# Feed-forward strips of gate and up as seven block products instead of eight

## The chip, the cores and the metric

The kernel runs on one core of a Trainium2 chip. The metric is the time of one execution on the device, in microseconds (us). TensorE multiplies matrices (PE in the profile, its weight loads PEld), VectorE (DVE) and ScalarE (ACT) work on elements, GpSimd (POOL) does little here, and SyncE (SP) issues the DMAs that bring weights from memory.

## The reference, cut to what matters

Two transformer blocks over 512 tokens of width 1024 in fp32. There are three feed-forwards of hidden width 2816. The first (f = 0) has a causal convolution between its products and is not touched. The second and third (f = 1 and f = 2) are the gated ones of the second block:

```python
def swiglu(h, w_gate, w_up, w_down):
    return (jax.nn.silu(h @ w_gate) * (h @ w_up)) @ w_down
```

Before each stands a norm with a shift and a scale that come from a product of the conditioning vector with `w_mod`, which the kernel calls `mod`.

## The kernel before

Activations lie transposed: features on the 128 partitions, 512 tokens along a row. Each fp32 operand is cut in a high part (fp32r, a copy by ScalarE) and a low part (the rest, a subtraction by VectorE). A product of two operands is three matmuls: high by high, high by low, low by high (`three`). All accumulate in one bank of `ps`.

The work is a fixed list of 'units'. A unit is one strip of weights, 128 output features by all input tiles (8 tiles of 128), times 512 tokens: 8 x 3 = 24 matmuls with 512 columns each into bank u % 2. The 22 hidden tiles of a feed-forward come in three parts of 8, 8 and 6. A part does for each hidden tile t a gate strip and an up strip, then the 8 strips of the down product over the hidden tiles of the part (`FF_PARTS`, stage names `(f, "up", part)` and `(f, "down", part)`).

The loop bodies per hidden tile are:

- SP loads strip u into slot u % 4 of `w_raw` when unit u - 4 is done.
- ScalarE `cut_hi(u + 2)` and `cut_hi(u + 3)` copy strips to `w_hi`; it takes silu of the gate's bank into `t_b`, and later copies `t_b` to `y_hi`.
- VectorE `cut_lo(u + 2)` and `cut_lo(u + 3)` subtract into `w_lo`; it multiplies `t_b` by the up bank and subtracts `y_lo = t_b - y_hi`.
- TensorE runs `unit(u)` and `unit(u + 1)`. It waits for the strip's low part (`lo_cut`) and for its bank having been read (`bank_read`).

In the down stage VectorE adds each strip's bank to `x` (`residual`). In f = 1, part 0, VectorE also sums up the third group of `mod` there (`mod_sum`), and after the norm `mix2`, which follows f = 1, it sums the fourth. For that TensorE turns tiles of `mod_acc` (`mod_turn(3)`, 16 transposes) just behind the totals of that norm, and then runs `keep_busy(6, 0)`, six idle matmuls of 256 columns, until the first normed tile is there.

Each engine works through its own list in order. Nothing but semaphores ties them. The two buffers `w_raw` and `w_lo` of a slot share their memory, so the low part is written over the raw strip.

## Time and profile before

| | |
|---|---|
| time, median of 3 runs | 1790.01 us (1788.58 to 1790.34) |
| time of the profiled execution | 1788.7 us |
| its span, first to last instruction | 1786.8 us |
| granted TensorE clock | 1.000 of full speed |
| PE busy, share of the span | 99% |
| DVE busy | 56% |
| ACT busy | 38% |

The span is what the trace shows between the first and the last instruction of the core, and the time of an execution is 1.9 us more. In the views a group's duration is that of one instruction from its start to its modelled end. Instructions of one engine overlap at their edges, so what one costs in a packed stream is the distance from its start to the next one's start.

### The profile page before, as it was taken

How to read it: one execution, taken by the hardware profiler on the slowest of the kernel's cores; microseconds unless marked ns; L12 is line 12 of the kernel's file. 1: busy time of each engine (PE TensorE's matmuls, PEld its weight loads, DVE VectorE, ACT ScalarE, POOL GpSimd, SP SyncE). 2: the span in 40 equal slices, each digit the busy share in tenths (PEclk: the TensorE clock that was granted, in tenths of full speed). 3: DMA queues.
4: the chain of work that ended last, by engine and by line, in shares of the span. 5: the costliest groups of instructions: out<-in, count | busy, mean ns of one | idle time of the engine just before them, and what ended most of it. 6: DMA issues, size and time to landing. Idle time of an engine off the chain costs nothing. (4 is left out here: it accounts for less than half of the span.)

```text
span 1786.8 us, 20550 instructions
## 1 busy us (share of the span) xinstructions
PE 1775.4 (99%) x8453; PEld 1480.8 (83%) x8453; DVE 992.1 (56%) x1384; ACT 676.4 (38%) x1041; POOL 23.4 (1%) x54
## 2 busy tenths in 40 slices
PE   8999999999999999999999999999999999999999
PEld 8888888887888888888888888888888888888887
DVE  5755553457787766684433333768878633333333
ACT  5544441334323322352222222465666432122222
POOL 0000000000000000000000000001100000000000
PEclk9999999999999999999999999999999999999999
DMA  5323232355586555333233333232221333333333
GB/s 161 112 85 92 83 86 86 102 187 165 191 260 227 193 188 192 94 96 102 86 102 95 95 95 91 74 83 60 55 64 36 95 106 95 96 101 98 94 89 100
DMA packets 326609, 201.64 MB, mean 113 GB/s; under 512 B 7112, under 2 KB 315766, under 8 KB 326518
## 3 DMA queue, kind: packets, MB, share of 16 engines
q1 hardware_dynamic: 326082, 199.52, 37.3%
q8 instruction: 67, 1.10, 0.3%
q0 software_dynamic: 192, 0.52, 0.1%
q10 hardware_dynamic: 244, 0.30, 0.0%
q14 instruction: 24, 0.20, 0.0%
HBM read 196.39 MB, written 2.10 MB: 111 GB/s over the span
## 5 line engine op out<-in xcount | busy, mean ns | idle before, releaser
L1560 PE MATMUL ps<-u_hi,w_hi 128*128 128x512 f32 (+1 forms) x1664 | 647.8, 390 | 4.6 <-DVE u_lo L1119 2.1
L1560 PE MATMUL ps<-u_hi,w_lo 128*128 128x512 f32 (+1 forms) x1656 | 641.3, 387 | 0.0
L1560 PE MATMUL ps<-u_lo,w_hi 128*128 128x512 f32 (+1 forms) x1664 | 637.9, 387 | 0.0
L955 DVE TENSOR_TENSOR w_lo<-w_raw,w_hi 128x1024 fp32r<-128x1024 f32 (+2 forms) x306 | 363.3, 1187 | 244.0 <-ACT w_hi L511 242.6
L511 ACT ACTIVATE w_hi<-w_raw 128x1024 fp32r<-128x1024 f32 (+2 forms) x307 | 314.6, 1025 | 236.3 <-DMA w_raw<-in_w_down 80.0
L1560 PEld LDWEIGHTS ps<-u_hi,w_hi 128*128 128x128 f32 x1664 | 312.5, 188 | 70.2 <-DVE w_lo L955 4.6
L1560 PEld LDWEIGHTS ps<-u_lo,w_hi 128*128 128x128 f32 x1664 | 312.6, 188 | 62.4
L1560 PEld LDWEIGHTS ps<-u_hi,w_lo 128*128 128x128 f32 x1656 | 310.9, 188 | 63.7
L1560 PE MATMUL ps<-y_hi,w_hi 128*128 128x512 f32 (+1 forms) x662 | 257.1, 388 | 0.0
L1560 PE MATMUL ps<-y_hi,w_lo 128*128 128x512 f32 (+1 forms) x662 | 256.4, 387 | 0.0
L1560 PE MATMUL ps<-y_lo,w_hi 128*128 128x512 f32 (+1 forms) x662 | 256.3, 387 | 0.0
L1560 PEld LDWEIGHTS ps<-y_hi,w_lo 128*128 128x128 f32 x662 | 124.3, 188 | 25.4
L1560 PEld LDWEIGHTS ps<-y_lo,w_hi 128*128 128x128 f32 x662 | 124.3, 188 | 25.2
L1560 PEld LDWEIGHTS ps<-y_hi,w_hi 128*128 128x128 f32 x662 | 124.3, 188 | 25.1
L720 ACT ACTIVATE y_hi<-t_b 128x512 fp32r<-128x512 f32 x66 | 41.8, 633 | 239.8 <-DVE t_b L1309 239.8
L1032 DVE SCALAR_TENSOR_TENSOR x<-ps,gains,x 128x512 f32<-128x512 f32 (+1 forms) x59 | 42.5, 723 | 138.1 <-PE ps L1560 138.1
L1309 DVE TENSOR_TENSOR t_b<-t_b,ps 128x512 f32<-128x512 f32 x66 | 45.2, 685 | 111.9 <-PE ps L1560 111.9
L1093 DVE SCALAR_TENSOR_TENSOR mod_acc<-mod_raw,c_act,mod_acc 128x1024 f32<-128x1024 f32 x63 | 80.7, 1281 | 3.4 <-DVE mod_acc L1093 0.5
L717 ACT ACTIVATE t_b<-ps 128x512 f32<-128x512 f32 x44 | 26.4, 599 | 138.5 <-PE ps L1560 138.5
L1311 DVE TENSOR_TENSOR y_lo<-t_b,y_hi 128x512 fp32r<-128x512 f32 x66 | 45.7, 693 | 46.1 <-ACT y_hi L720 46.1
L545 ACT ACTIVATE t_b<-x 128x512 f32<-128x512 f32 x28 | 17.7, 632 | 83.8 <-DVE x L1030 47.2
L1030 DVE TENSOR_TENSOR x<-x,ps 128x512 f32<-128x512 f32 (+1 forms) x34 | 22.1, 654 | 33.2 <-PE ps L1560 32.8
(290 smaller groups left out, 1319.6 us busy)
## 6 DMA issues: line engine op xcount, KB each, us to landing
mod_raw<-in_w_mod SPq DMA_DIRECT2D x72, 512.0 KB, 4.8
w_raw<-in_w_in SPq DMA_DIRECT2D x71, 512.0 KB, 3.9
w_raw<-in_w_ffn_up SPq DMA_DIRECT2D x44, 512.0 KB, 3.9
w_raw<-in_w_gate SPq DMA_DIRECT2D x44, 512.0 KB, 3.8
w_raw<-in_w_up SPq DMA_DIRECT2D x44, 512.0 KB, 3.8
w_raw<-in_w_down SPq DMA_DIRECT2D x32, 512.0 KB, 3.8
w_raw<-in_w_ffn_down SPq DMA_DIRECT2D x16, 512.0 KB, 3.8
w_raw<-in_w_down SPq DMA_DIRECT2D x16, 384.0 KB, 3.4
```

The costliest lines, as they stand in the source:

```text
L511: e.activation(w_hi[u % SLOTS][:, 0:n_k, :], w_raw[u % SLOTS][:, 0:n_k, :], ACT.Copy).then_inc(hi_cut, 1)
L545: e.activation(t_b[c % 2][:, :], x[:, c, :], ACT.Square).then_inc(squared, 1)
L717: e.activation(t_b[j][:, :], ubank(u), ACT.Silu).then_inc(bank_read[u % 2], 1)
L720: e.activation(y_hi[:, t, :], t_b[j][:, :], ACT.Copy).then_inc(y_hi_set, 1)
L955: e.tensor_tensor(w_lo[u % SLOTS][:, 0:n_k, :], w_raw[u % SLOTS][:, 0:n_k, :], f32(w_hi[u % SLOTS][:, 0:n_k, :]), ALU.subtract).then_inc(l ...
L1030: ins = e.tensor_tensor(x[:, c, cols], x[:, c, cols], src[:, cols], ALU.add)
L1032: ins = e.scalar_tensor_tensor(out=x[:, c, cols], in0=src[:, cols], scalar=gain(c), in1=x[:, c, cols], op0=ALU.mult, op1=ALU.add)
L1093: e.scalar_tensor_tensor(out=acc, in0=r, scalar=c_act[:, k:k + 1], in1=acc, op0=ALU.mult, op1=ALU.add).then_inc(mod_taken, 1)
L1309: e.tensor_tensor(t_b[j][:, :], t_b[j][:, :], ubank(u + 1), ALU.mult).then_inc(bank_read[(u + 1) % 2], 1)
L1311: e.tensor_tensor(y_lo[:, t, :], t_b[j][:, :], f32(y_hi[:, t, :]), ALU.subtract).then_inc(y_lo_set, 1)
L1560: return e.matmul(out_, lhsT, rhs, start=start, stop=stop, skip_group_check=skip)
```

## The change

Of the 44 pairs of gate and up strips in f = 1 and f = 2, 29 (`PAIRS`) are computed in another way. The two strips are seen as a 2 x 2 block matrix: gate or up, times upper or lower half of the input features (`KH` = 4 tiles each). The activations are 2 x 2 blocks too: upper or lower half of the features, times first or second half of the tokens (256 columns). The four result blocks then come from seven block products (Winograd's form of Strassen's scheme) in place of eight. Each product is 4 x 3 = 12 matmuls of 256 columns. For it sums of weight blocks (four a pair) and sums of activation blocks (four a feed-forward, `t_raw`) are formed, cut in high and low parts, and results are added after.

The pairs run in five runs, one each in f = 1 parts 1 and 2 and in f = 2 parts 0, 1 and 2, of 7, 5, 5, 7 and 5 pairs. Before each run one regular tile (three in f = 2, part 0) stays (`PLAIN_TILES`). Two sets of pair buffers alternate. Set 1 lies on the memory of the four weight slots, so its first load waits for the last regular unit, and the down strips' first loads wait for the run's last but one pair. The products 4 and 3 of a pair are issued after 1 and 2 of the next one. Those of a run's last pair are issued within its first down unit.

`mod_turn(3)` moves from the norm `mix2` to a place before the last down unit of f = 1, part 0; the sums of `mod`'s fourth group move there too, since the activation sums take the memory of `mod_acc`. `keep_busy` of that norm grows from 6 to 20. The waits on unit counters are rewritten with helpers (`units_before`, `banks_read`, `slot_loads`) that leave the paired units out; this changes no order elsewhere.

The core of the diff:

```diff
+PLAIN_TILES = {1: (8, 1, 1), 2: (3, 1, 1)}
+RUNS = [(f, p) for f in (1, 2) for p in range(3) if PLAIN_TILES[f][p] < FF_PARTS[p]]
+PAIRS = [(f, p, t) for f, p in RUNS for t in range(PLAIN_TILES[f][p], FF_PARTS[p])]
...
         def sync(e):
+            def load_gate(q):
...
+                name, c, _, _ = UNITS[PAIR_UNIT[q]]
+                e.dma_start(entries(st_raw[n], spot(q).w11, 2).rearrange("p (k n) -> p k n", n=P), strip(PAIR_UNIT[q])).then_inc(gate_in[n], 16)
...
+            def load_pairs(run):
...
+                    e.wait_ge(t_set, 4)
+                load_gate(first)
+                load_up_top(first)
+                load_up_bottom(first)
+
+                e.wait_ge(unit_done, units_before(PAIR_UNIT[first]))
+                load_gate(first + 1)
+                load_up_top(first + 1)
+                load_up_bottom(first + 1)
+                load_gate(first + 2)
+                for q in range(first + 2, last + 1):
+                    load_up_top(q)
+                    if q < last:
+                        load_gate(q + 1)
+                    load_up_bottom(q)
...
         def scalar(e):
+            def pairs(f, part):
+                first, last = FIRST_PAIR[f, part], LAST_PAIR[f, part]
+                for q in range(first, last + 1):
+                    if q > first:
+                        part_sums(q)
+                        part_second(q)
+                    e.wait_ge(product_done, nth_product(q, 1))
+                    if q:
+                        e.wait_ge(up_1, q)
+                    e.activation(q1_sb, pair_bank(q, 0), ACT.Copy).then_inc(kept, 1)
+                    part_last(q)
+                    if q < last:
+                        part_gate(q + 1)
+                    e.wait_ge(gates_set, nth_half(q, 0))
+                    e.activation(pair_tile(q)[:, half(0)], pair_tile(q)[:, half(0)], ACT.Silu).then_inc(hidden_act, 1)
+                    if q == last:
+                        cut_hi(U[f, "down", part])
+                    if q > first:
+                        second_silu(q - 1)
+                    e.wait_ge(product_done, nth_product(q, 6))
+                    if q > 1:
+                        e.wait_ge(gates_set, nth_half(q - 2, 1))
+                    e.activation(t_sb(q), pair_bank(q, 0), ACT.Copy).then_inc(kept, 1)
...
+                    if q > first:
+                        finish(q - 1)
+                    e.wait_ge(product_done, nth_product(q, 5))
+                    e.activation(q1_sb, pair_bank(q, 2), ACT.Copy).then_inc(kept, 1)
...
         def vector(e):
+            def pairs(f, part):
+                first, last = FIRST_PAIR[f, part], LAST_PAIR[f, part]
+                for q in range(first, last + 2):
+                    before, ahead = q > first, q <= last
+                    last_sum = f == 2 and part == 0 and q == first
+                    if before:
+                        up_second(q - 1)
+                    if before and ahead:
+                        add_last(q)
+                    if q - 2 >= first:
+                        low_hidden(q - 2)
+                    if before and ahead:
+                        part_second(q)
+                        part_sums(q)
+                    if ahead:
+                        first_gate(q)
+                        part_last(q)
+                    if before:
+                        up_first(q - 1)
+                        second_gate(q - 1)
+                    if q < last:
+                        part_gate(q + 1)
...
+                    if before:
+                        hidden(q - 1)
+                    if q < last:
+                        add_strips(q + 1)
...
         def tensor(e):
+            def product(q, n, dst, left, right, start):
+
+                for k in range(KH):
+                    ins = three(pair_bank(q, dst), (left[0][:, k, :], left[1][:, k, :]), (right[0](k), right[1](k)), start and k == 0, True, skip=True)
+                ins.then_inc(product_done, 1)
...
+                for q in range(first, last + 1):
...
+                    product(q, 1, 0, (hi[:, spot(q).w11, :, :], lo[:, spot(q).low11, :, :]), block_of(0, 0), True)
+                    product(q, 2, 1, (hi[:, spot(q).w12, :, :], lo[:, spot(q).low12, :, :]), block_of(KH, 0), True)
+                    if q > first:
+                        fourth_product(q - 1)
+                        third_product(q - 1)
...
+                    product(q, 6, 0, (hi[:, spot(q).s2, :, :], hi[:, spot(q).s2_raw, :, :]), sum_of(1), False)
...
+                    product(q, 5, 2, (hi[:, spot(q).s1, :, :], lo[:, spot(q).s1, :, :]), sum_of(0), True)
...
+                    product(q, 7, 0, (hi[:, spot(q).s3, :, :], lo[:, spot(q).s3, :, :]), sum_of(2), False)
...
+                        if f == 1 and part == 0 and c == KC - 1:
+                            mod_turn(3)
...
             total("mix2")
-            mod_turn(3)
-            keep_busy(6, 0)
+            keep_busy(20, 0)
```

What VectorE's steps are, with the elements of a row: `add_strips` three sums of 512, `add_last` one of 512, `part_gate`, `part_sums` and `part_last` one subtraction of 1024 each, `part_second` one of 512, `up_second`, `first_gate` and `second_gate` one sum of 256 each, `up_first` and `hidden` one product of 256 each, and `low_hidden` a subtraction of 512. In the regular tile before a run `beside_plain` does `add_strips`, `add_last`, `part_gate`, `part_second` and `part_sums` of the first pair, ahead of that tile's own multiplication. The activation sums (`whole`, `token_sum`, `token_low`: four of each, 1024 elements) stand beside the down units of f = 1, part 0, and around the three regular tiles of f = 2, part 0.

## Rows read from the trace of the kernel before

**Rows 1.** The page: busy time of each engine; granted clock in 40 slices

```profile
PE 1775.4 (99%) x8453; PEld 1480.8 (83%) x8453; DVE 992.1 (56%) x1384; ACT 676.4 (38%) x1041; POOL 23.4 (1%) x54
...
PEclk9999999999999999999999999999999999999999
```

**Rows 2.** TensorE's waits, the longest: us in total, times, longest

```profile
PE ps L1560 <- DVE u_lo L1119: 2.1, 1, 2.1
```

**Rows 3.** Chain that ended last, a piece of f = 2: start us, us, what

```profile
1420.22 334.86 PE ps L1560 x1476
```

**Rows 4.** Timeline, last unit, columns halved: start us, us, engine, instruction

```profile
1778.30 0.28 PE L1560 MATMUL ps<-y_lo,w_hi 128*128 128x256 f32 x1
1778.30 0.19 PEld L1560 LDWEIGHTS ps<-y_hi,w_lo 128*128 128x128 f32 x1
...
1780.20 0.28 PE L1560 MATMUL ps<-y_hi,w_lo 128*128 128x256 f32 x1
```

**Rows 5.** Timeline of TensorE early in the kernel, columns halved

```profile
27.26 0.28 PE L1560 MATMUL ps<-u_lo,w_hi 128*128 128x256 f32 x1
...
29.88 0.28 PE L1560 MATMUL ps<-u_hi,w_lo 128*128 128x256 f32 x1
```

**Rows 6.** VectorE's groups by form: count, busy us, mean ns, idle before

```profile
L955 DVE TENSOR_TENSOR w_lo<-w_raw,w_hi 128x1024 fp32r<-128x1024 f32 x274 | 334.8, 1222 | 211.4 <-ACT w_hi L511 210.4
L1093 DVE SCALAR_TENSOR_TENSOR mod_acc<-mod_raw,c_act,mod_acc 128x1024 f32<-128x1024 f32 x63 | 80.7, 1281 | 3.4 <-DVE mod_acc L1093 0.5
L1311 DVE TENSOR_TENSOR y_lo<-t_b,y_hi 128x512 fp32r<-128x512 f32 x66 | 45.7, 693 | 46.1 <-ACT y_hi L720 46.1
...
L1359 DVE TENSOR_TENSOR v_hi<-ps,v_hi 128x256 fp32r<-128x256 f32 x16 | 6.0, 419 | 1.0 <-ACT v_hi L759 0.8
...
L1032 DVE SCALAR_TENSOR_TENSOR x<-ps,gains,x 128x256 f32<-128x256 f32 x6 | 2.7, 481 | 6.1 <-PE ps L1560 6.1
```

**Rows 7.** Timeline of VectorE: packed pairs of instructions, in two stages

```profile
706.30 1.22 DVE L955 TENSOR_TENSOR w_lo<-w_raw,w_hi 128x1024 fp32r<-128x1024 f32 x1 [1.65 <-ACT w_hi L511]
707.44 0.68 DVE L1309 TENSOR_TENSOR t_b<-t_b,ps 128x512 f32<-128x512 f32 x1
...
1156.26 2.48 DVE L1049 TENSOR_REDUCE mod<-ps 128x4 f32<-128x512 f32 x4
```

**Rows 8.** ScalarE's groups by form

```profile
L511 ACT ACTIVATE w_hi<-w_raw 128x1024 fp32r<-128x1024 f32 x275 | 289.6, 1054 | 231.6 <-DMA w_raw<-in_w_down 78.7 <-DMA w_raw<-in_w_ffn_down 41.8 <-DMA w_raw<-in_w_gate 35.1
...
L759 ACT ACTIVATE v_hi<-ps 128x256 fp32r<-128x256 f32 x16 | 5.3, 382 | 1.0 <-PE ps L1563 0.8
```

**Rows 9.** DMA issues: count, KB each, median us to landing; then slots until 40 us

```profile
w_raw<-in_w_gate SPq DMA_DIRECT2D x44, 512.0 KB, 3.8
...
w_raw<-in_w_attn_out SPq DMA_DIRECT2D x8, 256.0 KB, 2.8
...
DMA to landing us min/median/max: 3.7/6.7/9.8
```

**Rows 10.** Timeline of TensorE in the norm `mix2`

```profile
1144.03 1.91 PE L1563 MATMUL ps<-consts,mod_acc 128*128 128x128 f32 x16
1145.70 0.96 PE L1560 MATMUL ps<-mask_win,ones_r 128*128 128x256 f32 x6
1146.74 0.47 PE L1560 MATMUL ps<-u_hi,w_hi 128*128 128x512 f32 x1
```

**Rows 11.** Timeline of VectorE in the regular tiles of f = 2, part 0

```profile
1429.07 0.75 DVE L989 SCALAR_TENSOR_TENSOR u_lo<-t_a,mod,u_hi 128x512 fp32r<-128x512 f32 x1
1432.79 1.23 DVE L955 TENSOR_TENSOR w_lo<-w_raw,w_hi 128x1024 fp32r<-128x1024 f32 x1 [2.97 <-ACT w_hi L511]
...
1442.31 0.69 DVE L1309 TENSOR_TENSOR t_b<-t_b,ps 128x512 f32<-128x512 f32 x1 [2.63 <-PE ps L1560]
1443.70 0.69 DVE L1311 TENSOR_TENSOR y_lo<-t_b,y_hi 128x512 fp32r<-128x512 f32 x1 [0.70 <-ACT y_hi L720]
...
1453.19 0.69 DVE L1309 TENSOR_TENSOR t_b<-t_b,ps 128x512 f32<-128x512 f32 x1 [2.64 <-PE ps L1560]
```

More of the change, by code:

```diff
@@ L250, in two_blocks @@
             ctx.push(r1.pop_all())
+        pair_tiles(0, 16)
+        with ExitStack() as r2:
+            wholes = {1: [sb(f"u_whole{n}", [P, KH, SEQ], F32, r2) for n in range(2)]}
         with ExitStack() as r2:
@@ L701, in ffn @@
                     y0 = Y_FILL[f, part]
-                    for t in range(tiles):
+                    for t in range(PLAIN_TILES[f][part] if f else tiles):
                         j = t % 2
@@ L1042, in residual @@
                         mod_sum(2, c)
+                    if u0 == U[1, "down", 0]:
+                        if c == KC - 1:
+                            for k in range(MOD_BANKS[3]):
+                                mod_sum(3, k)
+                        beside_down(c)
                 if u0 == U[1, "down", 0]:
                     mod_finish(2)
+                    mod_finish(3)
             def mod_sum(g, k):
@@ new lines, in add_last, with beside_plain @@
+            def add_last(q):
+                n = pair_set(q)
+                e.wait_ge(blocks_summed, 2 * q + 1)
+                if q > 1:
+                    e.wait_ge(product_done, nth_product(q - 2, 3))
+                e.tensor_tensor(entries(st_raw[n], spot(q).s4), entries(st_sum[n], spot(q).s2_raw), entries(st_raw[n], spot(q).w12), ALU.add).then_inc(blocks_summed, 1)
+            def beside_plain(f, part, t):
+                sums = f == 2 and part == 0 and t == 2
+                if sums:
+                    token_sum(f, 2)
+                if (f, part) in RUNS and t == PLAIN_TILES[f][part] - 1:
+                    first = FIRST_PAIR[f, part]
+                    add_strips(first)
+                    add_last(first)
+                    if sums:
+                        token_low(f, 2)
+                    part_gate(first)
+                    part_second(first)
+                    part_sums(first)
@@ new lines, in behind_plain @@
+            def behind_plain(f, part, t):
+                if f == 2 and part == 0 and t == 0:
+                    whole(f, 2)
+                    whole(f, 3)
+                    token_sum(f, 0)
+                    token_sum(f, 1)
+                elif f == 2 and part == 0 and t == 1:
+                    token_sum(f, 3)
+                    token_low(f, 0)
+                    token_low(f, 1)
+            def pairs(f, part):
[20 more added lines that the diff above has]
+                        part_gate(q + 1)
+                    elif q == last:
+                        cut_lo(U[f, "down", part])
+                    if last_sum:
+                        token_low(f, 3)
+                    if before:
+                        hidden(q - 1)
+                    if q < last:
+                        add_strips(q + 1)
+                    elif q == last:
+                        cut_lo(U[f, "down", part] + 1)
+                low_hidden(last)
@@ L1294, in ffn @@
                     y0 = Y_FILL[f, part]
-                    for t in range(tiles):
+                    for t in range(PLAIN_TILES[f][part] if f else tiles):
                         j = t % 2
@@ L1335, in vector @@
             norm("mix2", U["gate_f"])
-            for k in range(MOD_BANKS[3]):
-                mod_sum(3, k)
-            mod_finish(3)
             p0 = U["proj"]
@@ L1802, in ffn @@
                         unit_pair(U[f, "up", 0], u_act, FILL[f"ffn{f}"] * KC)
-                    for t in range(2 if part == 0 else 0, 2 * tiles):
+                    for t in range(2 if part == 0 else 0, 2 * (PLAIN_TILES[f][part] if f else tiles)):
                         unit(U[f, "up", part] + t, u_act)
+                    if (f, part) in RUNS:
+                        pairs(f, part)
                     if f == 2 and part == 2:
```

433 lines of the change are left out of this document (368 added, 65 removed).

## The prediction

> **What bounds the kernel now.** I read the page first, then TensorE's waits, then the chain, then single stretches of the timeline. The page shows TensorE busy for 1775.4 of 1786.8 us, at the full granted clock in every slice [rows 1]; VectorE and ScalarE are busy for about half of the span or less. The reader should see that one engine is the bound. The waits agree: the longest that TensorE ever has is 2.1 us, at the very start [rows 2], and all its waits together are 8.3 us. In the chain the whole of f = 2 up to its last down strips is one piece of TensorE, 334.86 us for 1476 matmuls [rows 3]. So what counts is first how much time TensorE's own stream loses, and then whether any other engine can still follow.
>
> **TensorE's stream, the gain.** A piece of 1476 matmuls with 512 columns in 334.86 us is 0.2269 us for one [rows 3]. A regular pair of strips is 2 x 24 = 48 of them, 10.89 us. The new pair is 7 x 12 = 84 matmuls of 256 columns, each with weights of its own. The kernel has some of just this kind. In its last unit two of them stand 16 places apart, at 1778.30 and 1780.20, so one takes 0.1188 us [rows 4]; early in the kernel two stand 22 apart, at 27.26 and 29.88, 0.1191 us [rows 5]. Half the columns thus cost 0.52 of the time, not 0.50. With 0.119 a new pair takes 10.00 us. The gain is 0.89 us a pair, and 29 x 0.894 = 25.9 us. A count of work alone, an eighth of 10.89, would have given 39.5 us; the third that is missing is what narrow matmuls lose.
>
> The weight load of one of these matmuls is shown 0.19 us long, more than the 0.119 us between matmuls [rows 4], and yet the stream doesn't slow down; loads overlap with the matmuls and with each other. The Trainium skill (TensorE: Matmul & The Clock Gate, Part 3, 'The mechanism') says that a weight load overlaps with running matmuls only where it is for another group of rows, which would speak against the change; the row contradicts it. The same page ('Back-to-back issue gap') gives N / 2.4 + 2.5 ns between matmuls. By it I estimate 48 x 215.8 - 84 x 109.2 ns = 1.19 us a pair and 34 us in all; the rows have 227 and 119 ns, and the sum goes by them.
>
> **What is moved onto the path.** `mod_turn(3)` stood in the norm `mix2`, where TensorE has nothing to do until the first normed tile. Its 16 transposes run from 1144.03 to 1145.70, 1.67 us [rows 10]. Now they stand between two down units of f = 1, in the full stream, and cost that and about 0.1 us for the restart of the matmuls: 1.8 us. In the norm `keep_busy(20)` fills 20 x 0.119 = 2.4 us from 1144.03 and ends at 1146.4; the first real matmul is at 1146.74 [rows 10]. So it costs nothing. VectorE's four reductions that leave that norm, 2.5 us [rows 7], had no one waiting, and I count nothing for them.
>
> **VectorE in a steady pair.** This is the term that can undo the change. VectorE's packed instructions overlap by 0.08 us: one of 1.22 us is followed after 1.14 [rows 7]. From the forms [rows 6] less 0.08, the three subtractions of 1024 cost 3 x 1.14; the three sums of `add_strips` 0.72 (its successor waits for it) + 0.61 + 0.61; `add_last`, `part_second` and `low_hidden` 3 x 0.61; the three small sums 3 x 0.35 and the two small products 2 x 0.40. Together 3.42 + 1.94 + 1.83 + 1.05 + 0.80 = 9.04 us, against TensorE's 10.00. It fits, with 0.96 to spare.
>
> Does the order of its list allow it? Let TensorE start product 1 of pair q at 0, and each product take 1.43. A result can be read 0.33 us after its last slot. Product 7 of pair q - 1 can be read at 0.3. Then `up_second` to `up_first` cost 0.35 + 0.61 + 0.61 + 0.61 + 1.14 + 0.35 + 1.14 + 0.40 = 5.21, until 5.5. `second_gate` has to wait for product 3, readable at 5.7 + 0.3 = 6.0. It and `part_gate`, `hidden` and `add_strips` cost 3.83, until 9.9; the next product 7 can be read at 10.3. Both idle times are short, 0.5 and 0.4 us. TensorE's own needs come later than VectorE's results: product 4 at 2.9 wants `up_second` (0.7), product 6 at 5.7 wants `part_second` (2.6), the next product 1 at 10.0 wants `part_gate` (7.7). The nearest is product 7 at 8.6. It wants ScalarE's copy of product 6's bank, readable at 7.5, copied by 7.9; the copy stands behind `second_silu`, which ends at 6.0 + 0.42 + 0.39 = 6.9. So 0.7 us are left. ScalarE's own sum is about 5.5 us: three copies of 1024 at 0.96, two of 512 at 0.54, five small ones at 0.3 [rows 8]. I take a steady pair at 10.00.
>
> **The edges of the five runs.** Here other engines do show.
>
> - Set 1 lies on the weight slots, so the second pair's gate strip is asked for only when the last regular unit is done. It lands after 3.8 us [rows 9]; ScalarE's `part_gate` makes that 4.9, the silu and the copy of product 6 behind it 5.7. Product 7 of the first pair is due after four products, at 5.7. I take 0.1 us a run, 0.5 in all.
> - f = 1, part 1: VectorE comes late from the down units. Behind the last one it has `residual` 0.67, four reductions 2.5, two `token_low` 2.3 and two `mod_finish` of about 0.5, 6.0 to 6.5 us, and then 5.5 us of preparation before the regular tile's multiplication. ScalarE's copy of product 1 is queued behind that tile's `y_hi`. Product 6 then waits for 0.3 us.
> - f = 2, part 0: four `whole`, four `token_sum` and three `token_low` stand before the run. The first two `whole` fit into 2.97 us of idle time [rows 11]. The next four sums move the second tile's multiplication from 1442.3 to 1443.0, `y_lo` then ends at 1445.0, three more bring VectorE to 1448.5. From there `token_sum` 1.14, `add_strips` 1.94, `add_last` 0.61, `token_low` 1.14 and `part_gate` 1.14 end at 1454.5. Product 1 is due at about 1453.0, just ahead of the third multiplication at 1453.19 [rows 11]. TensorE waits for 1.5 us, and for 0.4 again at product 6: 1.9.
> - Ends of the runs: from product 3 of the last pair 0.33 + 0.42 + 0.39 + 0.48 + 0.63 + 0.69 and five hand-overs of 0.03 make 3.1 us to `y_lo`. In the parts of 6 tiles it is covered by 12 matmuls, 2.7 us: 0.4 us each, twice. In those of 8 tiles 15 matmuls, 3.4 us, cover it.
>
> Sum: 0.5 + 0.3 + 1.9 + 0.8 = 3.5 us. Bounds: nothing, if VectorE is a little quicker everywhere; three times as much, some 10 us, if each edge has one more instruction of 1.2 us in front. The down strips that follow a run are asked for a whole pair ahead, 10 us against 3.8, and cost nothing.
>
> **The number.** 25.9 - 1.8 - 3.5 = 20.6 us less. The profiled execution took 1788.7 us (1786.8 of span and 1.9 around it), the median of the runs 1790.0, 1.3 more. 1788.7 - 20.6 + 1.3 = 1769.4, and I say 1769.5.
>
> **Rivals.**
>
> A. VectorE doesn't overlap here, because nearly each of its instructions waits for another engine's semaphore. Then full durations count: 3 x 1.222 + 6 x 0.693 + 3 x 0.419 + 2 x 0.481 = 10.05, with 14 hand-overs of 0.03 10.5 us [rows 6]. VectorE becomes the bound by 0.5 us a pair, in the pairs of a run behind its second, 19 of them: + 9.5, 1779. For it speaks how little is spare; against it the packed instruction in [rows 7], which also had a semaphore. The Trainium skill (VectorE: DVE Perf Modes, 'Terms') has a flush behind each operation, the next one starting only when the pipe is empty, which would be this case; the 1.14 us after a 1.22 us instruction disagree.
>
> B. The first loads of set 1 pile up. The second pair's gate strip has two halves of the up strip and another gate strip right behind it on the queue. In the pile-up at the start of the kernel a slot took 6.7 us at the median, up to 9.8 [rows 9]. 2.9 us more in each of five runs are + 14.5, 1784. Against it: the gate strip is the first of them.
>
> C. Slower than before: VectorE waits for ScalarE within the pair. If two of its six subtractions find the copy just begun, 1.05 us each [rows 8] on top of 10.5 without overlap, a pair takes 12.6 on VectorE, 2.6 over TensorE, + 49 us: 1819. It decides from 10.0 + 20.6 / 19 = 11.1 us a pair: below, the kernel is still faster. ScalarE's 5.5 us a pair speak against it.
>
> D. Weight loads do bind in a long stream: 84 x 0.188 = 15.8 us a pair, 4.9 more than now, + 142 in place of - 25.9. The longest stream of such matmuls in the rows is 23, so it isn't quite excluded.
>
> E. No change that can be measured: A and B together, 1793.5 at their full size, near 1790 at most of it.
>
> **Chances.** The forecast, 1766 to 1775, has 66 in 100; A 11, B 10, C 7, D 2, E 4. The range 1765 to 1782 takes in the forecast, A, and B to half its size, about 82 in 100. For this kernel 0.2%, 3.6 us, is about what a measurement can tell from no change. Faster by more: 66 + 11 + 10 = 0.87. Within it 0.04, slower 0.09.
>
> **What would show it.** In the profile after, matmuls of 256 columns in f = 1 and f = 2 at 0.119 us from start to start, and a steady pair of 10.0 us from product 1 to product 1. VectorE near 90% busy in a run, idle before `up_second` and `second_gate` and nowhere else for long. TensorE's new waits only at the run's first and last products, longest in f = 2, part 0, for `part_gate`. A pair of 10.5 us or more, with TensorE waiting before product 7 in each, would be A or C; a wait of 2 us or more before each run's first product 7 would be B.

## The result, and the profile after

The changed kernel takes 1764.27 us, the median of 4 runs (1762.52 to 1765.21), against 1789.45 us for the kernel before in the same session: a ratio of 0.9858, 95% interval 0.9841 to 0.9875, 25.2 us less. The forecast was 1769.5 with a range from 1765 to 1782. The sign was right, and so was where the gain and the losses come from; the size of the gain in TensorE's stream was not, and the time lies 0.7 us under the range. Span against span, 1786.8 became 1760.5 us: 26.3 less, where the working had 20.6. The nine executions of this kernel on record took from 1762.42 to 1768.17 us, four of them over 1765.

The page of the changed kernel, its lines for [rows 1]:

```profile
PE 1746.4 (99%) x9511; PEld 1502.7 (85%) x9511; DVE 1170.5 (66%) x1698; ACT 766.5 (44%) x1223; POOL 23.4 (1%) x54
...
PEclk9999999999999999999999999999999999999999
```

TensorE is still the bound, at the full granted clock throughout. 1058 matmuls were added (29 pairs of 84 narrow ones in place of 48 wide ones, and 14 of keep-busy), and its busy time fell by 29 us. VectorE has 178 us more work.

TensorE's waits in the changed kernel, for [rows 2]: the longest of all, then those from the block products (us in total, times, longest):

```profile
PE ps L2044 <- DVE u_lo L1461: 2.1, 1, 2.1
...
PE ps L2044 <- DVE st_lo L1635: 1.4, 1, 1.4
...
PE ps L2044 <- ACT t_a L978: 0.9, 4, 0.4
...
PE ps L2044 <- ACT t_a L965: 0.4, 1, 0.4
```

The last three are new, and none is long. The first of them is product 1 of f = 2, part 0, for `part_gate`; the second is four runs' first product 7, for ScalarE's copy of product 6; the third is product 6 of f = 2, part 0. A wait in this view counts from the modelled end of the matmul before. What the stream loses is the distance of two starts beyond the usual one, and it is larger: 1.6, 1.6 and 0.5 us for the three. Times of waits below are of this second kind unless they are read from a view.

Now the stream itself. Five stretches of 20 us, one inside each run; the number to read is the count of matmuls (x) that TensorE shows in each. A matmul that reaches over an edge counts too, so some 2 are to be taken off:

```profile
960.00:980.00 20.00, 20.00 (x178) 1.00 0.27 80
1070.00:1090.00 20.00, 20.00 (x172) 1.00 0.31 90
1460.00:1480.00 20.00, 20.00 (x172) 1.00 0.29 83
1580.00:1600.00 20.00, 20.00 (x179) 1.00 0.34 96
1690.00:1710.00 20.00, 20.00 (x179) 1.00 0.32 90
```

TensorE is busy the whole time in each and the clock is the same, yet three stretches hold 178 or 179 matmuls and two hold 172. The starts in the trace give 0.1133 us from start to start for the first sort, 0.1178 for the second. 0.1133 is half of the 0.2267 that a wide matmul takes. A product of 12 takes 1.36 or 1.41 us, a pair 9.52 or 9.90. The first matmuls of product 1 in two neighbouring pairs stand 84 matmuls apart, here for the faster rate (f = 2, part 1) and the slower (f = 1, part 2):

```profile
1557.23 0.28 PE L2044 MATMUL ps<-u_hi,st_hi 128*128 128x256 f32 x1
...
1566.75 0.28 PE L2044 MATMUL ps<-u_hi,st_hi 128*128 128x256 f32 x1
```

```profile
1055.85 0.28 PE L2044 MATMUL ps<-u_hi,st_hi 128*128 128x256 f32 x1
...
1065.75 0.28 PE L2044 MATMUL ps<-u_hi,st_hi 128*128 128x256 f32 x1
```

Neither rate is the 0.119 of the prediction. Of the intervals in the five runs some 1400 are of the faster sort and some 1010 of the slower.

The sum by stages, from the starts in the two traces: f = 1 (first to last matmul) 361.6 to 350.9 us, 10.7 less, against 8.0 predicted; f = 2 up to the second down unit of its last part 334.5 to 317.8, 16.6 less before rounding, against 12.6; what lies ahead of f = 1 and between the two is 1.2 longer (the longest piece of that, 0.5 us, is a transfer of `w_o` that took 4.31 us and not 3.81). -10.7 - 16.6 + 1.2 = -26.1, against 26.3 from the spans; the rest is rounding.

### The profile page after: what moved, and what is told of

It is laid out like the page before. It is cut to its first block and busy times, and to the rows that moved or that the text cites. A ratio compares the mean times of both kernels' runs of the same rounds, so it can differ in the third digit from the quotient of the medians.

```text
span 1760.5 us, 23555 instructions
## 1 busy us (share of the span) xinstructions
PE 1746.4 (99%) x9511; PEld 1502.7 (85%) x9511; DVE 1170.5 (66%) x1698; ACT 766.5 (44%) x1223; POOL 23.4 (1%) x54
## 5 line engine op out<-in xcount | busy, mean ns | idle before, releaser
L2044 PE MATMUL ps<-u_hi,w_hi 128*128 128x512 f32 (+1 forms) x1200 | 468.1, 391 | 3.8 <-DVE u_lo L1461 2.1
L2044 PE MATMUL ps<-u_hi,w_lo 128*128 128x512 f32 (+1 forms) x1192 | 461.4, 387 | 0.0
L2044 PE MATMUL ps<-u_lo,w_hi 128*128 128x512 f32 (+1 forms) x1200 | 458.0, 387 | 0.0
L1251 DVE TENSOR_TENSOR w_lo<-w_raw,w_hi 128x1024 fp32r<-128x1024 f32 (+1 forms) x248 | 292.3, 1179 | 115.6 <-ACT w_hi L718 114.4
L718 ACT ACTIVATE w_hi<-w_raw 128x1024 fp32r<-128x1024 f32 (+1 forms) x249 | 253.4, 1020 | 202.5 <-DMA w_raw<-in_w_down 71.0
L2044 PE MATMUL ps<-t_hi,st_hi 128*128 128x256 f32 x580 | 137.5, 279 | 1.3 <-ACT t_a L978 0.9
L2044 PE MATMUL ps<-t_lo,st_hi 128*128 128x256 f32 x464 | 129.1, 278 | 0.0
L1635 DVE TENSOR_TENSOR st_lo<-st_raw,st_hi 128x1024 fp32r<-128x1024 f32 x87 | 105.9, 1218 | 14.1 <-ACT st_hi L916 13.7
L2044 PEld LDWEIGHTS ps<-t_hi,st_hi 128*128 128x128 f32 x580 | 100.8, 188 | 3.1 <-issue 2.8
L2044 PE MATMUL ps<-u_hi,st_hi 128*128 128x256 f32 x348 | 96.9, 278 | 1.4 <-DVE st_lo L1635 1.4
```

Of the source, the lines that this page charges most:

```text
L718: e.activation(w_hi[u % SLOTS][:, 0:n_k, :], w_raw[u % SLOTS][:, 0:n_k, :], ACT.Copy).then_inc(hi_cut, 1)
L1251: e.tensor_tensor(w_lo[u % SLOTS][:, 0:n_k, :], w_raw[u % SLOTS][:, 0:n_k, :], f32(w_hi[u % SLOTS][:, 0:n_k, :]), ALU.subtract).then_inc(l ...
L1635: e.tensor_tensor(out_, raw, f32(hi), ALU.subtract).then_inc(part_lo, 1)
L2044: return e.matmul(out_, lhsT, rhs, start=start, stop=stop, skip_group_check=skip)
```

## The experiments

**1. The changed kernel again.** No edit.

> The changed kernel once more, nothing edited. Its pair runs show two rates for a matmul of 256 columns, 0.1133 us and 0.1178 us from start to start, each kept over dozens to hundreds of matmuls and changed only behind a gap of TensorE (run f=1 part 1: 0.1178 up to its first product 7, then 0.1133; f=1 part 2: 0.1178 throughout; f=2 part 0: 0.1133 between products 1 and 6, then 0.1178; f=2 parts 1 and 2: 0.1133 from the first product 7). Theory R (the rate is drawn anew at each restart of the stream): the same five runs show another pattern of the two rates, and the span differs from 1760.5 by up to some 2 to 5 us. Theory P (the rate belongs to the place: strips, banks, the length of the gap in front): the same pattern again within a matmul or two, and a span within 1 us of 1760.5.

The span was 1764.3 us, 3.8 more, and the pattern was another one. The same five places:

```profile
960.00:980.00 20.00, 20.00 (x173) 1.00 0.29 82
1070.00:1090.00 20.00, 20.00 (x172) 1.00 0.29 83
1460.00:1480.00 20.00, 20.00 (x172) 1.00 0.33 94
1580.00:1600.00 20.00, 20.00 (x172) 1.00 0.38 108
1690.00:1710.00 20.00, 20.00 (x179) 1.00 0.28 79
```

In the first and the fourth place, 178 and 179 matmuls have become 173 and 172. From product 1 of the first pair to the last block product, the down unit's wide matmuls in between left out, the five runs add up to 287.7 us instead of 283.6. 4.1 us here explain the 3.8 of the span. So the rate doesn't belong to the place, and theory P falls. Theory R is not contradicted yet.

**2. A drain before each pair.** In the list of TensorE:

```diff
                         e.wait_ge(pair_hidden, q - 1)
+                    if q > first:
+                        e.wait_ge(product_done, nth_product(q - 1, 7))
```

> The changed kernel with one wait more: before product 1 of every pair but a run's first, TensorE waits until its own product 7 of the pair before is complete. That forces a gap of about 0.2 to 0.4 us in each of 24 places and a restart behind it. Theory R (rate drawn at each restart): within one run some pairs go at 0.1133 us (84 matmuls in 9.52 us) and others at 0.1178 (9.90 us), mixed; span 1760.5 + 24 x 0.3 = about 1768, give or take 4. Theory P (rate fixed by the place, above all by which gap stood in front): all pairs with the same forced gap in front go at the same rate, so 24 equal pairs; a span of about 1765 if all are fast, 1773 if all are slow.

The span was 1770.2 us. Each of the 24 forced gaps is 0.425 to 0.430 us from start to start. Neither theory fits. Behind its first pair f = 1, part 1 goes at 0.1178 throughout, and the other four runs at 0.1133. In 22 of the gaps the rate from before returns, after at most five matmuls. In two it doesn't: the last twelve matmuls of the first pair go at 0.1178 in f = 2, parts 0 and 1, and those behind the gap at 0.1133. So a gap of TensorE's own seldom changes the rate, but it can. The other changes in this profile and in the two before stand behind waits for another engine or behind wide matmuls; that such a wait does more than a gap of TensorE's own was not tested alone.

**3. A shift instead of a gap.**

```diff
+                    if q > first:
+                        mm(pair_bank(q, 0)[:, 0:64], hi[:, spot(q).w11, 0, :], u_hi[:, 0, 0:64], True, True)
                     product(q, 1, ...
```

> The changed kernel with one matmul of 64 columns more ahead of product 1 of every pair but a run's first; it writes into the bank that product 1 then starts over. No wait and no gap, only a shift of phase, 24 times. Theory R in its narrow form (only a gap with a foreign wait changes the rate): runs keep one rate from a gap to the next, as before, and the span is 1760.5 to 1764.3 plus 24 x 0.03 to 0.05, some 1762 to 1766. Theory R in its wide form (any shift draws the rate anew): within a run pairs at 9.5 and pairs at 9.9 us are mixed.

The span was 1766.0. The rate now changes within a run; stretches of four pairs of f = 2, part 1, all busy throughout:

```profile
1558.00:1568.00 10.00, 10.00 (x87) 1.00 0.41 115
1569.50:1578.50 9.00, 9.00 (x82) 1.00 0.40 117
1579.50:1588.00 8.50, 8.50 (x74) 1.00 0.45 125
1599.50:1608.00 8.50, 8.50 (x77) 1.00 0.21 62
```

For the last two, of equal length, 74 and 77 matmuls are the slower and the faster rate. The rate changes at one odd matmul of 64 columns, in either direction, though not at each. The wide form of theory R holds. Only a third of the matmuls were at the faster rate, so nothing is won.

**4. Narrow matmuls without the algorithm.** The kernel before, its 58 strips issued by halves of the columns:

```diff
+                if u in NARROW:
+                    for h in range(2):
+                        for k in range(KC):
+                            left, right = (w_hi[c][:, k, :], w_lo[c][:, k, :]), acts(k)
+                            ins = three(ubank(u)[:, half(h)], left, (right[0][:, half(h)], right[1][:, half(h)]), k == 0, k == KC - 1)
```

> The kernel before, with the same 58 strips (29 pairs) computed as before, by eight block products' worth of work, but each matmul of 512 columns issued as two of 256, first all of the lower half of the columns, then all of the upper: 96 narrow matmuls a pair instead of 48 wide ones. No sums of blocks, no new work on the other engines. Theory W (the width alone sets the price, at either of two rates): 96 x 0.1133 = 10.88 us a pair where the stream is at the fast rate, as much as the 48 wide ones at 0.2267, and 96 x 0.1178 = 11.31 where it is slow; the kernel then takes 0 to 12.5 us more than before. The prediction's own figure, 0.119, gives 11.42 a pair and 15.5 us more. Rival (the two rates come from the pair's own waits and operands): one steady rate here, the same in all five stretches.

1808.2 us against 1788.8, a span of 1806.3. All five stretches run at one rate:

```profile
960.00:980.00 20.00, 20.00 (x169) 1.00 0.36 105
...
1580.00:1600.00 20.00, 20.00 (x169) 1.00 0.36 105
```

That is 0.1200 us a matmul and 11.52 a pair. Against half a wide matmul each, the 2784 narrow ones cost 2784 x (0.1200 - 0.1133) = 18.6 us more; the span rose by 19.5. It is a third rate, slower than both of the pairs. Theory W falls, at least in its 'at either of two rates'. The rival is right that the stretches are alike, but doesn't say why they are slower.

**5 and 6. Bursts by themselves.** The kernel before, with 24 bursts of 96 narrow matmuls behind one up unit of f = 0. Their core, here for kind 1:

```python
for i in range(96):
    k, s, prod = i // 3 % 8, i % 3, i // 12
    w = (hi[:, k, :], hi[:, k, :], lo[:, k, :])[s]
    mm(bank(5)[:, cols], w, (u_hi, u_lo, u_hi)[s][:, k, cols], True, True)
```

> The kernel before, with a measurement put into one up unit of f = 0 (the third strip pair's gate strip of part 1): behind its own 24 matmuls TensorE issues 24 bursts of 96 matmuls of 256 columns on the strip and tokens that it already has, into banks 5 to 7, where nothing reads them; the output of the kernel is not changed. Six kinds of burst, four times each, every burst behind a complete drain and one odd matmul of 64, 112, 160 or 208 columns that shifts its phase: (0) high, high, low weights by eight token blocks, three banks in turn, as the block products do; (1) the same into one bank; (2) one and the same weight block and token block; (3) high and low weights of one block in turn, one token block; (4) one weight block, eight token blocks in turn; (5) eight weight blocks in turn, one token block. Theory A (what is read and written decides the rate): each kind has one rate of its own whatever the phase, and the kinds differ among 0.1133, 0.1178 and 0.1200 us. Theory R (phase decides): all kinds show the same set of rates, and which one comes goes with the odd matmul in front. If both: kinds 0 and 1 change with the odd matmul, and kind 2 doesn't. About 2304 x 0.117 = 270 us more than before in any case.

> The kernel before with the same place for bursts of 96 narrow matmuls as in the first measurement, where all 24 bursts settled at 0.1200 us whatever they read and wrote and whatever stood in front. Two things that the block products have were absent there: a semaphore raised by every twelfth matmul (a product's end) and waits on semaphores, already fulfilled, between the products. Six kinds, four bursts each, all with the products' order and three banks: (0) every twelfth matmul raises a semaphore; (1) one fulfilled wait before every twelfth; (2) both, with two waits; (3) every third matmul raises a semaphore; (4) no semaphore, weights taken from the tokens' tiles, another part of the memory; (5) no semaphore, one matmul of 256 columns more in front. Theory S (the semaphores of a product let the stream leave 0.1200): kinds 0 to 3, or those with a wait, run at 0.1133 or 0.1178, kinds 4 and 5 at 0.1200. Theory M (where the weights lie): kind 4 differs and the others are at 0.1200. If all are at 0.1200, what sets the pairs' two rates is neither of these, and stays open.

All 48 bursts ended at 0.1200 us (2073.6 and 2074.9 us of span): three banks or one, one weight block or eight, with semaphores raised or waited for, and with weights out of `u_hi` too. Behind the odd matmul up to eight matmuls came at about 0.118, then 0.1200 for the rest. Theory A in its first form, theory R for these operands, theory S and theory M all fall. One difference between the pairs and the narrow stretches at 0.1200 was left that could be tested: in which byte their tiles begin.

**7. Where the operands begin.** The same bursts, without semaphores, all operands out of `u_hi` and `u_lo`:

```diff
+                    w_at, t_at = ((16, 0), (32, 0), (48, 0), (64, 0), (16, 16), (0, 16), (8, 0), (4, 0))[kind]
+                        w = (u_hi, u_hi, u_lo)[s][:, k, w_at:w_at + P]
+                        a = (u_hi, u_lo, u_hi)[s][:, k, t_at:t_at + HALF]
```

> Bursts of 96 narrow matmuls in the same place as in the two measurements before, all with weights read out of the tokens' tiles and no semaphore. Eight kinds, four bursts each, that differ only in where, counted in bytes from the tile's start, weights and tokens begin: weights at 64, 128, 192 or 256 with tokens at 0; both at 64; weights at 0 and tokens at 64; weights at 32 and at 16 with tokens at 0. In the layout of the changed kernel the strips' tiles of the block products start 64 bytes off the tokens' tiles, modulo 128; w_hi and w_lo don't. Theory G (the grain of 128 bytes): kinds with an odd multiple of 64 between weights and tokens (first, third and sixth) run at 0.1133 or 0.1178, the others of 64 bytes' grain (second, fourth, fifth) at 0.1200; for the 32 and 16 bytes it says nothing. Rival: where the operands start has no effect, all at 0.1200.

One burst of each of the first six kinds, in the order of the list (an element has 4 bytes); the third window is 10 us long, and its burst is the one of that kind at 0.1133:

```profile
572.50:583.50 11.00, 11.00 (x95) 1.00 0.00 0
619.50:630.50 11.00, 11.00 (x95) 1.00 0.00 0
702.00:712.00 10.00, 10.00 (x90) 1.00 0.01 2
714.00:725.00 11.00, 10.94 (x92) 1.00 0.00 0
762.00:773.00 11.00, 10.94 (x92) 1.00 0.00 1
809.00:820.00 11.00, 11.00 (x94) 1.00 0.01 1
```

Windows of 11 us hardly tell 0.1178 from 0.1187, so the rates are from the starts, over the last 60 matmuls of each burst: weights at 64 and tokens at 0 0.1178 in four of four; weights at 192 0.1178 in three and 0.1133 in one; weights at 0 and tokens at 64 0.1178. Weights at 256 and tokens at 0, or both at 64, 0.1200 in all eight. The theory missed one kind: weights at 128 took 0.1187 on average, in an uneven rhythm. Those at 32 and 16 bytes, for which nothing was said, took 0.1183. So a distance of an odd multiple of 64 bytes gives the pairs' two rates, and a distance of 0 or 256 gives the third. The grain is not simply 128.

**8. The pairs, aligned.** The changed kernel with its strip tiles 64 bytes elsewhere:

```diff
-        pair_tiles(1, 80)
+        pair_tiles(1, 64)
...
-        pair_tiles(0, 16)
+        pair_tiles(0, 32)
```

> The changed kernel with its two sets of strip tiles moved by 64 bytes, so that they start at the tokens' place modulo 128: the pads in front of them are 64 and 32 elements instead of 80 and 16. Nothing else. Theory G: every matmul of the pairs takes 0.1200 us, a pair 10.08 us, and the five runs about 29 x 10.08 + 1.9 of waits = 294 us, against 283.6 to 289.3 in the three profiles of the changed kernel; a span of 1769 to 1771, which is where the prediction stood with its 0.119. Rival: the same two rates as before and a span of 1760 to 1766.

1770.6 us, span 1768.7. The five runs add up to 292.6 us:

```profile
960.00:980.00 20.00, 20.00 (x170) 1.00 0.28 80
1070.00:1090.00 20.00, 20.00 (x170) 1.00 0.28 80
1460.00:1480.00 20.00, 20.00 (x170) 1.00 0.36 103
1580.00:1600.00 20.00, 20.00 (x170) 1.00 0.37 106
1700.00:1720.00 20.00, 20.00 (x170) 1.00 0.28 82
```

The two rates are gone in all five. But the edit didn't align both sets. In the program's memory map the distance between strips and tokens, modulo 512 bytes, is 64 for both sets in the changed kernel; in this run it is 0 for set 1 and 128 for set 0. That is one kind of experiment 7 each, and each set keeps its own rate behind the first pairs: set 1 is at 0.1200 us, set 0 at 0.1186 in the uneven rhythm that weights at 128 had there (0.1187). The first matmuls of product 1 in three neighbouring pairs stand 10.04 and 10.00 us apart (9.99 by the rounded starts):

```profile
1560.20 0.28 PE L2044 MATMUL ps<-u_hi,st_hi 128*128 128x256 f32 x1
...
1570.24 0.28 PE L2044 MATMUL ps<-u_hi,st_hi 128*128 128x256 f32 x1
...
1580.23 0.28 PE L2044 MATMUL ps<-u_hi,st_hi 128*128 128x256 f32 x1
```

Theory G in its plain form (0.1200 for each distance that is a multiple of 128) is wrong for set 0, and so the span falls just below the 1769 to 1771 expected and the runs' sum is 1.4 below 294. The 17 pairs of set 0 are worth 17 x 84 x 0.0014 = 2.0 us of that. A pair at 10.00 to 10.04 us is what the prediction priced, at 10.00. The two pads, moved by 16 elements each, are worth 2.6 to 8.2 us by the spans.

**9. The other way round.** The kernel of experiment 4 with the weight slots an odd multiple of 64 bytes from the tokens:

```diff
+        sb("pad_w", [P, 16])
         w_hi = [sb(f"w_hi{n}", [P, KC, P], F32R) for n in range(SLOTS)]
...
+        sb("pad_x", [P, 16])
         x = sb("x", [P, KC, SEQ])
```

> The kernel before with the 29 pairs' matmuls issued as twice as many narrow ones, as measured already (0.1200 us each, 11.52 a pair, a span of 1806.3), and now with a pad of 64 bytes in front of the weight slots and another behind them, so that the weights start 64 bytes off the tokens modulo 128. Theory G: the narrow matmuls run at 0.1133 or 0.1178, a pair takes 10.88 or 11.31 us, and the span falls by 29 x 0.21 to 0.64 = 6 to 18 us, to between 1788 and 1800. Rival: 1806 again.

```profile
960.00:980.00 20.00, 20.00 (x172) 1.00 0.36 105
...
1580.00:1600.00 20.00, 20.00 (x172) 1.00 0.36 106
```

The narrow matmuls do fall to 0.1178, by 2784 x 0.0022 = 6.2 us; none of the five stretches reaches 0.1133. But the span rose from 1806.3 to 1809.8. The rest of this kernel's stream is of 512 columns and got slower; its 384 up matmuls of f = 0, part 0, from first to last:

```profile
547.89 0.39 PE L1563 MATMUL ps<-u_hi,w_hi 128*128 128x512 f32 x1
...
635.56 0.39 PE L1563 MATMUL ps<-u_hi,w_lo 128*128 128x512 f32 x1
```

That is 0.2289 us each, where the aligned slots give 0.2267. The expectation had left the wide ones out. Of the two layouts tried, the wide matmuls want the one and the narrow ones the other.

**10. VectorE's margin.** Two sums of 512 columns more per pair, feeding nothing:

```diff
+                if q not in FIRST_PAIR.values():
+                    for spare in (ssum, ssum_b)[:2]:
+                        e.tensor_tensor(spare[:, :], rstd[:, :], rstd[:, :], ALU.add)
```

> The changed kernel, with two additions of 512 columns more on VectorE in every pair but a run's first (24 pairs), ahead of its low part of the two strip sums; they add 1.22 us and feed nothing. The prediction's sum for VectorE is 9.04 us a pair; theory V says that this sum is right, so with 10.26 us VectorE becomes the bound and a pair takes 10.3 to 10.6 us (10.26 and the hand-overs that its semaphores cost), against 9.5 to 9.9 now: 24 x 0.5 to 0.8 = 12 to 20 us more, a span of 1773 to 1781. Rival A of the prediction (each instruction at its full length, 10.5 us a pair) would give 11.7 us and a span near 1805, but then the changed kernel could not have reached pairs of 9.52 us. If VectorE really needed much less than 9.04 us, the pairs would stay below 10 us and the span under 1768.

A span of 1768.2 us, below the 1773 to 1781 that theory V expected. Three pairs each of f = 2, part 1 and f = 1, part 1 (busy time of PE, PEld, DVE, ACT, POOL):

```profile
1583.30:1613.20 29.90, 29.43 (x255) 29.05 (x254) 29.80 (x49) 17.17 (x31) 0.00 (x0) 1.00 0.31 91
955.60:985.70 30.10, 29.87 (x254) 29.60 (x253) 30.00 (x49) 17.36 (x31) 0.00 (x0) 1.00 0.31 90
```

VectorE has 0.1 us of 30 idle: in these pairs it is the bound now, with 9.97 and 10.03 us a pair. Less the 1.22 added, its own list takes 8.75 to 8.8 us. The prediction's 9.04 was 0.3 too much. In the changed kernel itself three fast pairs look like this:

```profile
1578.10:1606.70 28.60, 28.60 (x255) 28.60 (x254) 26.72 (x43) 17.99 (x32) 0.00 (x0) 1.00 0.32 92
```

93% busy. The spare time is 0.7 us in a fast pair and 1.1 in a slow one.

**11. One part of the change alone.** The kernel before, with `mod_turn(3)` and its sums moved into the last down unit of f = 1, part 0, and `keep_busy(20)` in the norm:

```diff
+                        if f == 1 and part == 0 and c == KC - 1:
+                            mod_turn(3)
...
-            mod_turn(3)
-            keep_busy(6, 0)
+            keep_busy(20, 0)
```

> The kernel before with one part of the change alone: the 16 transposes of the last modulation group, with their four reductions and what ends them on VectorE, moved out of the norm mix2 to the last down unit of f = 1, part 0, and twenty matmuls of keep-busy in the norm in place of six. The prediction priced it at 1.8 us more (1.67 us of transposes and 0.1 of restart) and nothing in the norm. Theory: the span grows by 1.8 us and the norm keeps its length. Rival: the norm had waited for these transposes, or VectorE's four reductions of 2.5 us come in the way of the next part's first tiles: then the difference is 0 or less, or 2.5 and more.

1790.25 us against 1789.09; the span 1788.3, 1.5 more. The moved transposes and the norm:

```profile
907.49 0.39 PE L1560 MATMUL ps<-y_hi,w_lo 128*128 128x512 f32 x1
907.73 1.91 PE L1563 MATMUL ps<-consts,mod_acc 128*128 128x128 f32 x16
909.39 0.48 PE L1560 MATMUL ps<-y_hi,w_hi 128*128 128x512 f32 x1
...
1143.18 0.39 PE L1560 MATMUL ps<-y_hi,w_lo 128*128 128x512 f32 x1
...
1148.43 0.47 PE L1560 MATMUL ps<-u_hi,w_hi 128*128 128x512 f32 x1 [0.17 <-ACT u_hi L531]
```

1.66 us from the first transpose to the next real matmul, some 0.1 more for the restart. The norm takes 5.25 us from the last down matmul to its own first one, against 5.34 in the kernel before. One execution each couldn't show 1.8 us, since those of the kernel before spread over some 2; the lines above do. The term is right.

**12. The edges.** ScalarE's high part of the second pair's gate strip goes behind the silu in a run's first pair, and VectorE's third `token_low` behind the first pair's low parts:

```diff
-                    if q < last:
+                    if first < q < last:
                         part_gate(q + 1)
                     e.wait_ge(gates_set, nth_half(q, 0))
                     e.activation(..., ACT.Silu).then_inc(hidden_act, 1)
+                    if q == first:
+                        part_gate(q + 1)
...
-                    if sums:
-                        token_low(f, 2)
                     part_gate(first)
                     part_second(first)
                     part_sums(first)
+                    if sums:
+                        token_low(f, 2)
```

> The changed kernel with two instructions of its edges moved. ScalarE: in a run's first pair the high part of the second pair's gate strip goes behind the silu instead of in front of it. That strip lands 4.1 us after it is asked for, and the silu and the copy of product 6 no longer queue behind it; TensorE's waits before the first product 7 (0.32, 0.32, 0.52 and 0.41 us in four of the runs) should be gone. VectorE: in f = 2, part 0, the third token block's low part goes behind the low parts of the first pair; product 1 should wait 0.45 us instead of 1.6, product 6 still 0.5. Together 1.5 + 1.15 = 2.6 us less than the changed kernel: 1764.3 - 2.6 = 1761.7. Rival: the strip's low part, which VectorE makes behind the high part, comes later for the next product 1 and that waits instead; then only the 1.15 us are won. Both are smaller than what the two rates of the stream move from run to run, so the profile's waits decide, and the medians only lean.

> The changed kernel unedited, timed beside the one with the moved edges. Theory R: the single executions spread over some 1762 to 1767 us, as the profiled spans of 1760.5 and 1764.3 do, a spread that the kernel before (1788.6 to 1790.3) doesn't have; the median lies near 1764.3.

The edited kernel: 1762.27 us (1760.86 to 1763.45, 5 runs), ratio 0.9849, interval 0.9836 to 0.9863. The changed kernel beside it: 1764.67 (1762.42 to 1768.17, 4 runs), ratio 0.9865, interval 0.9852 to 0.9879. The intervals overlap, so the waits have to decide. The spread that theory R expected is there: 5.8 us over the changed kernel's four executions, 1.7 over nine of the kernel before beside them. Those of the edited kernel from the pairs:

```profile
PE ps L2046 <- ACT t_a L965: 1.5, 1, 1.5
...
PE ps L2046 <- DVE st_lo L1637: 0.3, 1, 0.3
```

The four waits for the copy of product 6 (line 978 in the changed kernel) are gone from the list, worth some 1.5 us from start to start. Product 1 of f = 2, part 0 waits for 0.3 us instead of 1.4. But product 6, which waited for 0.4, now waits for 1.5: nothing was won there. The timelines of ScalarE and VectorE show why:

```profile
1441.08 0.61 ACT L928 ACTIVATE st_hi<-st_sum 128x512 fp32r<-128x512 f32 x1
1445.47 0.63 ACT L1016 ACTIVATE y_hi<-t_b 128x512 fp32r<-128x512 f32 x1 [3.78 <-DVE t_b L1793]
1446.01 0.37 ACT L965 ACTIVATE t_a<-ps 128x256 f32<-128x256 f32 x1
```

```profile
1443.62 1.22 DVE L1338 TENSOR_TENSOR t_lo<-t_raw,t_hi 128x1024 fp32r<-128x1024 f32 x1
1444.76 0.68 DVE L1793 TENSOR_TENSOR t_b<-t_b,ps 128x512 f32<-128x512 f32 x1
```

Product 6 needs ScalarE's copy of product 1 (line 965). It is queued behind the regular tile's `y_hi`, which waits for VectorE's multiplication at 1444.76, and that stands behind the whole preparation, in whatever order it is. By these lines the wait would get shorter with fewer instructions in front of that multiplication, or with the copy ahead of `y_hi`; neither was run. The edited kernel has the lowest median here, by 2.4 us. By the waits ScalarE's edit is worth some 1.5 us and VectorE's nothing; more than that isn't shown.

## Why the prediction failed, point by point

- **TensorE's stream.** This is the step that failed, the term of 0.119 us for a narrow matmul, so 10.00 us a pair and a gain of 25.9. Measured: 0.1133 or 0.1178, 9.52 or 9.90 a pair. In the profile of the changed kernel the five runs took 283.6 us, their waits included, and 29 x 10.88 - 283.6 = 31.9 us less than before. The other two profiles have 287.7 and 289.3. The mechanism was right and the size was off, for a reason that [rows 4, 5] could not show on their face: they are of matmuls whose weights begin 256 bytes from the tokens' place, modulo 512, and both samples average their first eight or so matmuls at some 0.118 with the rest at 0.1200, as single intervals in the trace of before show. The change lays its strips 64 bytes off. Experiment 8, which takes that away, lands at 1770.6 with pairs of 10.00 to 10.04 us.
- **The range.** Its lower end, 1765, was 4.5 us under the forecast, with an edge cost of zero as the only gain. No bound was taken from below for the narrow rate, although 0.1133, half a wide matmul, was in the same rows; with it a pair costs 9.52 and the lower bound of the forecast lies 14 us lower. That the median fell just outside and not just inside is in part chance: which of the two rates a run of pairs gets differs from one execution to the next, and four of nine executions took more than 1765 us.
- **The formula for narrow matmuls.** The Trainium skill (TensorE: Matmul & The Clock Gate, 'Back-to-back issue gap') gives 109.2 ns for 256 columns by the formula that the prediction used, and states it for an isolated matmul. The faster rate here is 113.3 ns, so the formula missed it by 4 ns and the prediction's 119 by 6. No run shows 109.2, and one formula has no room for three rates.
- **A weight load of 0.19 us does not slow the stream.** Right: matmuls with weights of their own started every 0.1133 us over a whole run of pairs. Rival D did not come.
- **`mod_turn(3)` and `keep_busy(20)`.** Right, 1.8 us, shown alone in experiment 11.
- **VectorE.** Right in kind. The order of its list and its two short idle times, before `up_second` and `second_gate`, are there, at 0.26 and 0.27 us in a fast pair. The sum of 9.04 us was 0.3 high. Rival A needed 10.5 us a pair, rival C 12.6; experiment 10 gives 8.8.
- **The edges.** Predicted 3.5 us. Product 1 of f = 2, part 0 came 1.6 us late (1.5 predicted) and product 6 waited for 0.5 (0.4). Product 7 of the first pair waited for 0.3 to 0.5 us in four runs, not 0.1: the second pair's gate strip landed 4.1 us after it was asked for, not 3.8. The ends of the two 6-tile parts cost 0.4 us each as predicted. Product 6 of f = 1, part 1 waited for 0.1, not 0.3. In all some 4.6, 1.1 more. Rival B is the wait before product 7 with 2.9 us in each run, and did not come.

Against the working's own terms the profiled stream, its waits taken off, was 290.0 - 281.3 = 8.7 us quicker, the edges cost 1.1 more, and stretches without pairs 1.2 more: 6.4 less, where the spans show 5.7; 0.7 is left without a name. Why a distance of 64 bytes between weights and tokens changes the rate, and what chooses between 0.1133 and 0.1178, was not settled. Shown is that the distance does it, that the rate can change behind an odd matmul, and that it changed behind 2 of 24 gaps of TensorE's own. One regularity stands in the traces: in seven profiles with strips 64 bytes off, four runs each follow wide matmuls without a pause, and all 28 begin at 0.1178. 0.1133 was seen only behind a gap or an odd matmul.

## What to carry to other kernels

Price a new kind of instruction from one that stands in the same layout: for matmuls look where weights and tokens begin, and take single intervals, not the mean over a short burst. When a stream is the bound, count instructions in equal windows, since a busy share of 100% hides a rate that is 4 to 6% off. Read in the memory map where each buffer lies: a pad that was to align two sets here put one of them at another distance. And before an instruction is moved off a wait, follow each queue that the next wait depends on: the wait may only change its name.

## What the runs showed of the hardware

- A matmul of 256 columns with fp32r operands takes 0.1133 to 0.1200 us in a packed stream at the full granted clock (2.4 GHz); one of 512 columns 0.2267 or 0.2289. What counts is the distance between where weights and tokens begin. For 256 columns: 0 or 256 bytes (modulo 512) 0.1200; 128 bytes 0.1186 or 0.1187; 64 bytes, or another odd multiple of 64, 0.1133 or 0.1178. For 512 columns: 256 bytes 0.2267, an odd multiple of 64 0.2289. No run had both widths at their best with one layout for all; the changed kernel has, with one for each.
- The choice between 0.1133 and 0.1178 can last for hundreds of matmuls and differs from one execution to the next. The 5.6 us between three profiles of one kernel (1760.5, 1764.3, 1766.1) are this: their runs of pairs differ by 5.7. A difference of this size between two such kernels, seen in one profile each, is not yet an effect of the edit.
- Behind a gap of 0.4 to 0.6 us a narrow stream loses some 0.08 us beside the gap itself: the interval behind it is 0.193 us.
